# Moving a triangular substitution, its transposes and GpSimd's strip copies in the lead and the first turn of a fused decoder layer

## The chip, the cores and the metric

The kernel runs on one core of a Trainium2 chip. The metric is the device time of one execution in microseconds (us); lower is better.

## The reference

One layer for 512 tokens of width 1024, all in float32. The part at issue is the first of three stages: one projection feeds two token mixers, a differential attention of 8 heads and a chunked gated delta rule of 8 heads (chunks of 64 tokens, keys and values of 128):

```python
proj = rmsnorm(x, attn_norm[i]) @ w_in[i]
qa, ka, va, qb, kb, vb, zb, bb, ab, gl = jnp.split(proj, cuts, axis=-1)
...
probs = softmax(q @ k.T + bias)                  # two of them per head, causal, blocks of 128 rows
w = probs[:, :, 0] - lam * probs[:, :, 1]        # and w @ v
...
kkT = jnp.einsum('nbhid,nbhjd->nbhij', k_beta, k)
A = eye(64) + where(strict, kkT * decay, 0)      # one for each head and chunk: 64 of 64x64
sol = triangular_solve(A, rhs, lower=True, unit_diagonal=True)
...
x = x + (gates0 * (oa @ w_br_a) + gates1 * (ob @ w_br_b)) @ w_out
```

After it come a gated MLP with a short convolution and a gated projection of a per-layer input. The change does not touch them.

## The kernel before

**The projection as filling.** Weights come in chunks of 1024x128 in float32. GpSimd (`both`, L507 and L492) or ScalarE splits each into a high and a low part in a reduced format, and TensorE multiplies it as three products of 512 columns for each of 8 row blocks (`gemm`, L562). One such row block, three products, is one **step**, about 0.68 us. A `Fill` hands steps out, so that the code of TensorE is a list of small products, each behind a number of steps: `f.step(8)`. Four weight buffers turn; GpSimd begins chunk c when the product of chunk c-4 is done.

**Turns.** After the keys of all heads come `lead_turn`, then `turn(0)` to `turn(7)`. `turn(h)` holds the scan of the delta rule for head h and the attention of head h+1 (`a` in the code); `lead_turn` holds the attention of head 0. Each is written out four times, once for TensorE, ScalarE, VectorE and (the projection alone) GpSimd, as a fixed order for that engine; between engines there are only semaphores. Every engine works through its own list in order, so what stands behind a waiting instruction waits too.

**Attention of one head**, in four row blocks i, is a relay. TensorE: `scores(a, i)` (L698, the products of q and k into banks 3 and 4). VectorE: `maxima(a, i)` (L1705 adds the bias, L1710 takes the maxima). ScalarE: `softmax(a, i)` (L1152). VectorE: `combine(a, i)` (L1720 to L1722, the mixed probabilities into `pr`). TensorE: `turn_w(a, i)` (L705, transposes). ScalarE: `keep_w(a, i)` (L1158, into `wT`). `scores(a, i+1)` on TensorE wait for `keep_w(a, i)`. `prep` (L1675) scales q and k of the next head ahead of `scores(a, 0)`.

**The inverses of A.** The 64 matrices are inverted in blocks of 32. First all 128 diagonal blocks of 32x32 by columns on VectorE: `substitute(j0, j1)` does columns j0 to j1-1 of 31, two instructions each (L1810, L1812), and needs nothing from another engine. In the kernel before, the 31 columns are spread over `lead_turn`, between the maxima and the mixing. `turn_back` then transposes the result twice: into `dd` (L1817, semaphore `turned_back` 1) and into `li` (L1819, `turned_back` 2). From `dd` ScalarE places two strips (`place_rows`, L1274), from `li` two more (`place_columns`, L1289) and GpSimd the first two (L523). TensorE computes the blocks below the diagonal, `pair_low` (L756, L758) from `dd`, and, when ScalarE has copied them (`pair_copy`, L1324 and L1325), `pair_high` (L770, L772), from which `pair_sign` (ScalarE) and `pair_turn` (VectorE) fill further strips. Then the 64x64 blocks follow: `half_low(g)` (L785) and `half_high(g)` (L796), 8 matrices to a group, one group in each of turns 0 to 3, with `half_copy` and `half_take` on ScalarE between and behind. `half_take(g)` gives `xf_ready`, for which the first product of the scan of turn g waits (L899).

**GpSimd** copies its strips behind the first chunk that it splits for `stream.heads[0]`, and must wait there for `turned_back` 2:

```python
both(stream.heads[h].at(n))
if h == 0 and n == 0:
    pool.wait_ge(sem("turned_back"), 2)
```

**Two waits that the prediction speaks of.** `first_tap(a, 0)` on ScalarE (L1175) overwrites `qb`, and waits for `qeg`, which VectorE makes from `qb` in `turn` (L1891, behind `at_`, L1889):

```python
if n == 0:
    act.wait_ge(sem("qk"), h)
    act.wait_ge(sem("qeg"), h)
```

SyncE loads the rows for head 1 (`rows_of(1)`) between the second and third chunk of `stream.heads[0]`, and waits there for ScalarE's `first_decay` in the lead.

## Time and profile before

| what | us |
|---|---|
| median of 3 runs (1159.1 to 1159.82) | 1159.25 |
| the profiled execution | 1160.82 |
| its span, first to last instruction | 1159.0 |
| TensorE busy | 1123.9 |
| VectorE busy | 655.2 |
| ScalarE busy | 549.4 |
| GpSimd busy | 633.1 |

Times of the trace below are in the span's own microseconds: the lead begins at about 101 and turn 0 at 149.7. In a row, "[1.82 <-DVE pr L1722]" is the idle time of the engine just before, and what ended it. DVE is VectorE, ACT ScalarE, POOL GpSimd, PE TensorE, PEld its weight loads. A float32 matmul leaves two records, so 8 products show as x16. PEclk is the share of TensorE's full clock that was granted.

### The profile page before, as it was taken

What the parts mean: (1) busy time and instruction counts of PE and PEld (TensorE: products, weight loads), DVE (VectorE), ACT (ScalarE), POOL (GpSimd) and SP (SyncE); (2) the same over time, 40 slices, a digit from 0 to 9 for tenths busy, and PEclk for the clock granted to TensorE, in tenths of its full rate; (3) what the DMA queues carried; (4) which work ended last, traced back from release to release, by engine and by line L of the source; (5) the groups of instructions that cost most, each with busy time, mean ns of one, the idle gap of its engine ahead of it and who ended that gap; (6) DMA issues with size and microseconds to landing.
All of it is one profiled execution on the core that took longest, in us unless ns stands there. A gap on an engine that the chain in (4) does not pass through costs nothing.

```text
span 1159.0 us, 16765 instructions
## 1 busy us (share of the span) xinstructions
PE 1123.9 (97%) x5502; PEld 898.7 (78%) x5502; DVE 655.2 (57%) x1036; ACT 549.4 (47%) x886; POOL 633.1 (55%) x769
## 2 busy tenths in 40 slices
PE   6998989999999999999999999999999999999997
PEld 4786667777777777667878888888888888888886
DVE  4668976767666776862213324476776515731534
ACT  5584647566565656551322124544444314433542
POOL 6386264546554564645456554566576754573452
PEclk9999999999999999999999999999999999999999
DMA  8354031331404123213223523333333432332232
GB/s 243 77 132 130 26 94 35 85 85 35 102 18 118 38 64 100 75 54 85 79 77 105 181 72 91 91 93 114 103 90 91 116 102 73 109 96 80 74 89 79
DMA packets 196619, 104.36 MB, mean 90 GB/s; under 512 B 3926, under 2 KB 195401, under 8 KB 196553
## 3 DMA queue, kind: packets, MB, share of 16 engines
q1 hardware_dynamic: 196172, 103.39, 32.0%
q8 instruction: 34, 0.56, 0.2%
q14 instruction: 32, 0.26, 0.1%
q10 hardware_dynamic: 381, 0.15, 0.1%
HBM read 101.40 MB, written 2.13 MB: 89 GB/s over the span
## 4 chain that ended last, share of the span: by engine, by line
PE 87%; DVE 9%; ACT 3%; issue 1%; ACTq 0%; DVEq 0%
PE bank L562 75%; PE bank L698 2%; PE bank L712 1%; DVE prod L1810 1%; DVE xs L1812 1%; PE bank L705 1%; PE bank L657 1%; DVE pr L1722 1%; PE bank L922 1%; DVE pr L1721 0%; DVE oa_lo L1978 0%; PE bank L909 0%; PE bank L919 0%; PE bank L910 0%; PE bank L913 0%
## 5 line engine op out<-in xcount | busy, mean ns | idle before, releaser
L492 POOL TENSOR_TENSOR w_lo<-w_raw,w_hi 128x256 fp32r<-128x256 f32 x692 | 549.9, 828 | 259.9 <-ACT w_hi L1074 254.2
L562 PE MATMUL bank<-hn_hi,w_hi 128*128 128x512 f32 x1000 | 408.4, 408 | 1.0 <-DVE o_a L1985 1.0
L562 PE MATMUL bank<-hn_hi,w_lo 128*128 128x512 f32 x1000 | 391.0, 391 | 0.0
L562 PE MATMUL bank<-hn_lo,w_hi 128*128 128x512 f32 x1000 | 390.4, 390 | 0.0
L562 PEld LDWEIGHTS bank<-hn_hi,w_hi 128*128 128x128 f32 x1000 | 189.0, 189 | 43.7 <-issue 9.2
L562 PEld LDWEIGHTS bank<-hn_hi,w_lo 128*128 128x128 f32 x1000 | 187.9, 188 | 40.4
L562 PEld LDWEIGHTS bank<-hn_lo,w_hi 128*128 128x128 f32 x1000 | 188.7, 189 | 34.6 <-issue 1.7
L507 POOL CAST w_hi<-w_raw 128x1024 fp32r<-128x1024 f32 x70 | 78.2, 1117 | 222.0 <-PE bank L562 131.3
L1074 ACT ACTIVATE w_hi<-w_raw 128x1024 fp32r<-128x1024 f32 x111 | 117.9, 1062 | 77.6 <-PE bank L562 69.7
L2096 DVE SCALAR_TENSOR_TENSOR u<-vr,pt,u 128x511 f32<-128x511 f32 x88 | 88.9, 1010 | 8.3 <-DVE u L2096 0.7
L2090 DVE TENSOR_TENSOR vr<-bank,rs 128x512 f32<-128x512 f32 x44 | 30.4, 692 | 72.5 <-PE bank L562 67.1
L562 PE MATMUL bank<-fa_hi,w_hi 128*128 128x512 f32 x176 | 68.5, 389 | 0.0
L562 PE MATMUL bank<-fa_lo,w_hi 128*128 128x512 f32 x176 | 68.5, 389 | 0.0
L562 PE MATMUL bank<-fa_hi,w_lo 128*128 128x512 f32 x176 | 68.5, 389 | 0.0
L1536 ACT ACTIVATE u<-vr,pt 128x512 f32<-128x512 f32 x44 | 35.9, 816 | 38.2 <-DVEq L2091 37.5
L2130 DVE TENSOR_TENSOR x<-x,bank 128x512 f32 x16 | 11.0, 688 | 61.2 <-PE bank L562 60.5
L1541 ACT ACTIVATE fa_hi<-tn 128x512 fp32r<-128x512 f32 x22 | 13.9, 633 | 66.4 <-DVE tn L2108 66.4
L1152 ACT ACTIVATE pr<-bank,ast 128x128 f32<-128x128 f32 (+3 forms) x64 | 33.8, 528 | 19.9 <-DVE ast L1710 16.4
L2033 DVE TENSOR_TENSOR sg<-sg,bank 128x512 f32<-128x512 f32 x8 | 5.5, 687 | 62.8 <-PE bank L562 62.8
L1488 ACT ACTIVATE sg<-bank 128x512 f32<-128x512 f32 x12 | 7.2, 599 | 66.3 <-PE bank L562 66.3
L562 PEld LDWEIGHTS bank<-fa_lo,w_hi 128*128 128x128 f32 x176 | 33.0, 188 | 6.9
L562 PEld LDWEIGHTS bank<-fa_hi,w_lo 128*128 128x128 f32 x176 | 33.0, 188 | 6.9
(308 smaller groups left out, 1643.6 us busy)
## 6 DMA issues: line engine op xcount, KB each, us to landing
w_raw<-in_w_in SPq DMA_DIRECT2D x73, 512.0 KB, 6.7
w_raw<-in_w_up SPq DMA_DIRECT2D x44, 512.0 KB, 3.8
w_raw<-in_w_down SPq DMA_DIRECT2D x16, 512.0 KB, 3.9
crow<-cum_rows_out SPq DMA_DIRECT2D x16, 256.0 KB, 5.7
w_raw<-in_w_br_a SPq DMA_DIRECT2D x8, 512.0 KB, 4.0
w_raw<-in_w_br_b SPq DMA_DIRECT2D x8, 512.0 KB, 4.0
w_raw<-in_w_out SPq DMA_DIRECT2D x8, 512.0 KB, 3.9
w_raw<-in_w_ple_gate SPq DMA_DIRECT2D x8, 512.0 KB, 4.0
```

The source lines that it names most:

```text
L492: ins = pool.tensor_tensor(wlo[c.slot][:, ks, :], raw[c.slot][:, ks, :], whi[c.slot][:, ks, :].bitcast(F32), ALU.subtract)
L507: pool.tensor_copy(whi[c.slot][:, :, :], raw[c.slot][:, :, :]).then_inc(high_ready, 1)
L562: mm = pe.matmul(acc, w[c.slot][:, i, :], xx[:, x0 + i, :], start=(i == 0 and n == 0), stop=last)
L657: mm = pe.matmul(tiles(b)[:, t, :], key(h)[:, s], key(h)[:, s], start=True, stop=True)
L698: mm = pe.matmul(bank[3 + j][:, 0:(i + 1) * P], qa[s, i * P:(i + 1) * P], ka[s, 0:(i + 1) * P], start=True, stop=True)
L705: mm = pe.transpose(bank[3][:, t * P:(t + 1) * P], pr[0][:, t * P:(t + 1) * P], ident)
L1074: done(nc.scalar.activation(whi[c.slot][:, :, :], raw[c.slot][:, :, :], ACT.Copy), high_ready, c.number + 1)
L1152: done(nc.scalar.activation(pr[j][:, 0:w], bank[3 + j][:, 0:w], ACT.Exp, bias=ast[:, 2 + j:3 + j], scale=-1.0, accum_out=ast[:, 4 + j:5 + j]),
L1536: done(nc.scalar.activation(u[:, :], v[:, :], ACT.Identity, bias=col(PA_FBIAS + q * KF, f), scale=col(PA_TAP[2] + q * KF, f)), "u_made", 2 ...
L1541: done(nc.scalar.activation(fa_hi[:, 8 * FFN_HALF[part] + pair, :], tn[:, :], ACT.Copy), "fa_hi", f + 1)
L2090: done(V.tensor_tensor(v[:, :], bank[c.bank][:, :], rs[:, :], ALU.mult), bank_free[c.bank], c.uses + 1)
L2096: link(V.scalar_tensor_tensor(out=u[:, back:], in0=v[:, 0:T - back], scalar=col(PA_TAP[j] + q * KF, f), in1=u[:, back:], op0=ALU.mult, op1 ...
```

## The change

Four things, in one edit.

1. VectorE in the lead: `prep(0, 1)` goes ahead of the last instruction of `scale_rows`; the columns are spread behind the maxima with fewer in the lead (22 of 31), and the other 9 go into turn 0, around combine(1,0). `first_mask` goes behind `prep(1, 1)`.
2. VectorE in turn 0: maxima(1,0) come first; the transpose into `dd` comes behind column 30, maxima(1,1) ahead of the transpose into `li`; `at_` and `qeg` come behind both. The pair transposes and `key_decays(0)` go behind combine(1,2). TensorE's pair products, and ScalarE's strips and copies, move back in turn 0 accordingly, and `STEPS_FIRST` and the first steps of the lead are set anew.
3. Halves: the low half of group g+1 and the high half of group g are issued alternately in one group, `halves(g)`: `halves(-1)` and `halves(0)` in turn 0, then one in each of turns 1 to 3. `halves(3)` has the high half alone.
4. GpSimd's two strip copies go behind the fourth chunk of `stream.heads[0]`.

```diff
-STEPS_FIRST = ((2, 4, 1, 9, 1, 8, 1, 8), ((1, 1), (1, 1, 1), (1, 1, 1), (1, 1, 1)))
+STEPS_FIRST = ((2, 4, 1, 10, 1, 8, 1, 7), ((1, 1), (1, 1, 1), (1, 1, 1), (1, 1, 1)))
...
             for h in range(H - 2):
                 for n in range(len(TURN)):
                     both(stream.heads[h].at(n))
-                    if h == 0 and n == 0:
+                    if h == 0 and n == 3:
                         pool.wait_ge(sem("turned_back"), 2)
-                        pool.wait_ge(low_ready, stream.heads[0].at(0).number + 1)
+                        pool.wait_ge(low_ready, stream.heads[0].at(3).number + 1)
...
+            def low_half(m):
+                b = (5, 7)[m // 8 % 2]
+                at = slice(m % 8 * HEAD, (m % 8 + 1) * HEAD)
+                return pe.matmul(bank[b][UP, at], lt6[LOW, m, :], xf[LOW, m, UP], start=True, stop=True)
+
+            def high_half(m):
+                b = (5, 7)[m // 8 % 2]
+                at = slice(m % 8 * HEAD, (m % 8 + 1) * HEAD)
+                return pe.matmul(bank[b][LOW, at], lt6[UP, m, :], xf[UP, m, UP], start=True, stop=True)
+
+            def halves(g):
+
+                pe.wait_ge(sem("placed"), 2 if g < 0 else 6)
+                pe.wait_ge(sem("pairs"), 1 if g < 1 else 2)
+                if g >= 0:
+                    pe.wait_ge(sem("inverse_ui"), g + 3)
                 if g > 0:
                     pe.wait_ge(sem("ob_sum_read"), g)
                 for n in range(8):
-                    m = g * 8 + n
-                    mm = pe.matmul(bank[b][UP, n * HEAD:(n + 1) * HEAD], lt6[LOW, m, :], xf[LOW, m, UP],
-                                   start=True, stop=True)
-                mm.then_inc(sem("inverse_u"), 1)
...
+                    if g < H // 2 - 1:
+                        low = low_half(8 * g + 8 + n)
+                    if g >= 0:
+                        high = high_half(8 * g + n)
+                if g < H // 2 - 1:
+                    low.then_inc(sem("inverse_u"), 1)
+                if g >= 0:
+                    high.then_inc(sem("inverse_x"), 1)
```

TensorE's `lead_turn` and `turn`:

```diff
-                f.step(1)
+                f.step(2)
                 scores(0, 0)
                 f.step(6)
                 turn_w(0, 0)
...
-                f.step(before[1] - 2 if h == 0 else before[1])
+                f.step(before[1])
                 if h > 0 and halves_ob(h - 1):
...
-                if h == 0:
-                    for g in range(2):
-                        pair_low(g)
-                        f.step(1)
                 if attention:
                     turn_w(a, 0)
                 f.step(before[2])
                 if attention:
                     scores(a, 1)
+                if h == 0:
+                    f.step(6)
+                    pair_low(0)
+                    f.step(1)
+                    pair_low(1)
+                    f.step(2)
...
                 mm.then_inc(sem("vb_T"), 1)
-                if h == 0:
-                    f.step(before[3] - 5)
-                    pair_high(0)
-                    f.step(2)
-                    pair_high(1)
-                    f.step(3)
-                else:
-                    f.step(before[3])
+                f.step(before[3] - 9 if h == 0 else before[3])
                 if attention:
                     turn_w(a, 1)
                 f.step(before[4])
                 if attention:
                     scores(a, 2)
                     k_turn(a)
...
-                if h < H // 2:
-                    half_low(h)
-                f.step(before[5])
+                if 0 < h < H // 2:
+                    halves(h)
+                if h == 0:
+                    f.step(1)
+                    pair_high(0)
+                    f.step(2)
+                    pair_high(1)
+                    f.step(before[5] - 3)
+                else:
+                    f.step(before[5])
                 if attention:
                     turn_w(a, 2)
-                if h < H // 2:
-                    half_high(h)
                 f.step(before[6])
                 if attention:
                     scores(a, 3)
-                f.step(before[7])
+                if h == 0:
+                    f.step(3)
+                    halves(-1)
+                    f.step(3)
+                    halves(0)
+                    f.step(before[7] - 6)
+                else:
+                    f.step(before[7])
                 if more_a:
                     qk_sum(h + 2, 0, at("qa"))
```

ScalarE's `lead_turn` and `turn`:

```diff
                 prep_v(1, at("va"))
-                place_rows()
...
                     ob_r(h - 1)
-                if h == 0:
-                    pair_copy(0)
...
                     first_tap(a, 0, at("qb"))
                     softmax(a, 1)
                     if h == 0:
+                        place_rows()
+                        pair_copy(0)
+                        pair_copy(1)
+                    keep_w(a, 1)
+                    silu_exp(a, 0)
+                    if 0 < h < H // 2 - 1:
+                        half_copy(h + 1)
+                    if 0 < h < H // 2:
+                        half_take(h)
+                    softmax(a, 2)
+                    if h == 0:
                         pair_sign(0)
                         pair_sign(1)
-                    keep_w(a, 1)
-                    if h == 0:
+                        keep_w(a, 2)
                         place_columns()
-                    silu_exp(a, 0)
-                    if h < H // 2:
-                        half_copy(h)
-                    softmax(a, 2)
                     first_tap(a, 2, at("vb"))
                     head_exps(a)
-                    keep_w(a, 2)
-                    if h < H // 2:
-                        half_take(h)
+                    if h > 0:
+                        keep_w(a, 2)
                     k_copy(a)
+                    if h == 0:
+                        half_copy(0)
                     if more_a:
                         prep_qk(h + 2, 0, at("qa"))
                     square_q(a)
                     softmax(a, 3)
+                    if h == 0:
+                        half_copy(1)
+                        half_take(0)
                     silu_exp(a, 2)
                     keep_w(a, 3)
                     v_copy(a)
```

VectorE's `scale_rows`, `turn_back`, `lead_turn` and `turn`:

```diff
                 V.tensor_copy(wide(xs)[:, 0:SUB * SUB:SUB + 1], kzb[:, :])
+                prep(0, 1)
                 link(V.tensor_tensor(li[:, :, :], li[:, :, :], kzb[:, :].unsqueeze(2).to_broadcast([P, SUB, SUB]), ALU.mult))
...
                 done(V.transpose(dd[:, :, 0:SUB].rearrange("p n c -> p c n"), xs[:, :, :].rearrange("p i c -> p c i")),
                      "turned_back", 1)
+
+            def turn_again():
+
                 done(V.transpose(li[:, :, :].rearrange("p n i -> p i n"), xs[:, :, :]), "turned_back", 2)
...
-                prep(0, 1)
-                substitute(0, 3)
                 maxima(0, 0)
-                substitute(3, 5)
+                substitute(0, 2)
                 combine(0, 0)
-                substitute(5, 8)
+                substitute(2, 4)
                 maxima(0, 1)
-                substitute(8, 10)
+                substitute(4, 6)
                 combine(0, 1)
                 steps(conv(0, 0, at("qb")))
                 maxima(0, 2)
-                substitute(10, 12)
+                substitute(6, 8)
                 combine(0, 2)
                 steps(conv(0, 2, at("vb")))
                 maxima(0, 3)
                 steps(finish_silu(0, 0))
-                substitute(12, 13)
+                substitute(8, 9)
                 combine(0, 3)
-                substitute(13, 18)
+                substitute(9, 14)
                 prep(1, 0)
-                substitute(18, 24)
+                substitute(14, 20)
                 steps(finish_silu(0, 2))
                 attention_scale(0)
-                substitute(24, 28)
+                substitute(20, 21)
+                prep(1, 1)
+                substitute(21, 22)
                 first_mask()
-                prep(1, 1)
-                substitute(28, 31)
-                turn_back()
...
+                if h == 0:
+                    maxima(a, 0)
+                    substitute(22, 24)
+                    combine(a, 0)
+                    substitute(24, 31)
+                    turn_back()
+                    maxima(a, 1)
+                    turn_again()
+                    scaled_keys()
+                    combine(a, 1)
+                    scaled_values()
+                else:
+                    if attention:
+                        maxima(a, 0)
+                    if halves_ob(h - 1):
+                        low_ob(h - 1)
+                    scaled_keys()
...
-                    maxima(a, 0)
-                if h > 0 and halves_ob(h - 1):
-                    low_ob(h - 1)
...
-                if attention:
-                    combine(a, 0)
-                else:
-                    low_a(range(5, 7))
-                if h > 0:
-                    key_decays(h)
-                if attention:
-                    maxima(a, 1)
-                    if h > 0:
...
-                if attention:
-                    combine(a, 1)
+                    steps(conv(a, 0, at("qb")))
+                    maxima(a, 2)
+                    steps(finish_silu(a, 0))
+                    combine(a, 2)
                     if h == 0:
                         pair_turn(0)
                         pair_turn(1)
                         key_decays(h)
-                    steps(conv(a, 0, at("qb")))
-                    maxima(a, 2)
-                    steps(finish_silu(a, 0))
-                    combine(a, 2)
                     steps(conv(a, 2, at("vb")))
                     maxima(a, 3)
```

How the order moves on VectorE, at the end of the substitution and the beginning of turn 0. Before (L1810 and L1812 are a column, L1817 and L1819 the transposes, L1705 and L1710 maxima, L1720 to L1722 the mixing):

```order
L1810 TENSOR_TENSOR prod<-li,xs 128x31
L1812 TENSOR_TENSOR xs<-xs,prod 128x31
L1817 STREAM_TRANSPOSE dd<-xs 128x32x32
L1819 STREAM_TRANSPOSE li<-xs 128x32x32
L1705 TENSOR_TENSOR bank<-bank,bias 128x128 x2
L1710 TENSOR_REDUCE ast<-bank 128x1 x2
L1889 TENSOR_TENSOR at_<-bank,dec 128x512
L1891 TENSOR_TENSOR qeg<-qb,eg 128x512
L1720 RECIPROCAL ast<-ast 128x2
L1721 TENSOR_SCALAR pr<-pr,ast,sm 128x128
L1722 SCALAR_TENSOR_TENSOR pr<-pr,ast 128x128
L1705 TENSOR_TENSOR bank<-bank,bias 128x256 x2
```

Now (L1828 and L1830 a column, L1835 and L1840 the transposes, L1722 and L1727 maxima, L1737 to L1739 the mixing, L1905 and L1907 `at_` and `qeg`):

```order
L1828 TENSOR_TENSOR prod<-li,xs 128x60
L1830 TENSOR_TENSOR xs<-xs,prod 128x2x30
L1828 TENSOR_TENSOR prod<-li,xs 128x31
L1830 TENSOR_TENSOR xs<-xs,prod 128x31
L1835 STREAM_TRANSPOSE dd<-xs 128x32x32
L1722 TENSOR_TENSOR bank<-bank,bias 128x256 x2
L1727 TENSOR_REDUCE ast<-bank 128x1 x2
L1840 STREAM_TRANSPOSE li<-xs 128x32x32
L1905 TENSOR_TENSOR at_<-bank,dec 128x512
L1907 TENSOR_TENSOR qeg<-qb,eg 128x512
L1737 RECIPROCAL ast<-ast 128x2
L1738 TENSOR_SCALAR pr<-pr,ast,sm 128x256
```

`at_` and `qeg` stood between maxima(1,0) and combine(1,0), and stand now behind maxima(1,1) and both transposes, just ahead of combine(1,1).

ScalarE, from the first strips to the second kept row block. Before (L1274 `place_rows`, L1324 and L1325 pair copies, L1158 `keep_w`, L1175 `first_tap`, L1152 softmax):

```order
L1274 ACTIVATE o_a<-dd 32x32x32 x2
L1152 ACTIVATE pr,ast<-bank,ast 128x128 x2
L1324 ACTIVATE dd<-bank 32x16x32
L1325 ACTIVATE dd<-bank 32x16x32
L1324 ACTIVATE dd<-bank 32x16x32
L1325 ACTIVATE dd<-bank 32x16x32
L1158 ACTIVATE wT<-bank 128x128
L1200 ACTIVATE zb<-bank 128x512
L1203 ACTIVATE silu<-bank 128x512
L1163 ACTIVATE silu<-silu,sm 128x512
L1164 ACTIVATE silu<-silu 128x512
L1175 ACTIVATE qb<-bank,pt 128x512
```

Now, from the tap on (L1186 `first_tap`, L1163 softmax, L1285 `place_rows`, L1335 and L1336 pair copies, L1169 `keep_w(1, 1)`):

```order
L1186 ACTIVATE qb<-bank,pt 128x512
L1163 ACTIVATE pr,ast<-bank,ast 128x256 x2
L1285 ACTIVATE o_a<-dd 32x32x32 x2
L1335 ACTIVATE dd<-bank 32x16x32
L1336 ACTIVATE dd<-bank 32x16x32
L1335 ACTIVATE dd<-bank 32x16x32
L1336 ACTIVATE dd<-bank 32x16x32
L1169 ACTIVATE wT<-bank 128x2x128
L1202 ACTIVATE silu<-qb 128x512
L1174 ACTIVATE silu<-silu,sm 128x512
L1175 ACTIVATE silu<-silu 128x512
L1163 ACTIVATE pr,ast<-bank,ast 128x384 x2
```

The strips and the pair copies stood ahead of `keep_w(1, 0)`, and stand now between softmax(1,1) and `keep_w(1, 1)`.

## Rows read from the trace of the kernel before

**Rows 1.** The page, busy time of the engines.

```profile
PE 1123.9 (97%) x5502; PEld 898.7 (78%) x5502; DVE 655.2 (57%) x1036; ACT 549.4 (47%) x886; POOL 633.1 (55%) x769
```

**Rows 2.** Waits of PE, 60 to 151 us: total, times, longest.

```profile
PE bank L705 <- DVE pr L1722: 3.3, 2, 1.8
PE bank L698 <- DVE ka L1675: 1.9, 2, 1.1
```

**Rows 3.** Timeline of PE: start, us, engine, line.

```profile
149.69 0.49 PE L698 MATMUL bank<-ka,qa 64*128 64x128 f32 x4 [0.83 <-DVE ka L1675]
...
160.17 0.33 PE L705 MATMUL bank<-sq,pr 128*128 128x128 f32 x1 [2.09 <-DVE pr L1722]
```

**Rows 4.** Windows: length, busy PE, PEld, DVE, ACT, POOL, PEclk, DMA share, GB/s.

```profile
140.00:151.00 11.00, 10.17 (x44) 7.35 (x43) 10.07 (x28) 5.32 (x9) 0.00 (x0) 1.00 0.62 168
...
153.90:155.10 1.20, 1.14 (x64) 1.09 (x64) 0.00 (x0) 1.17 (x2) 1.00 0.00 0
...
160.00:161.00 1.00, 0.83 (x4) 0.66 (x4) 0.11 (x1) 0.45 (x3) 1.00 (x2) 0.79 0.00 0
161.00:164.00 3.00, 3.00 (x11) 1.75 (x10) 1.11 (x4) 2.34 (x4) 2.92 (x5) 0.50 0.20 48
```

**Rows 5.** Timeline of DVE, columns 22 to 30 and the mask between.

```profile
142.28 0.38 DVE L1810 TENSOR_TENSOR prod<-li,xs 128x207 f32<-128x207 f32 x1
...
148.16 0.69 DVE L1830 TENSOR_TENSOR dec<-dec,sq 128x512 f32<-128x512 f32 x1
...
150.98 0.19 DVE L1812 TENSOR_TENSOR xs<-xs,prod 128x31 f32<-128x31 f32 x1
```

**Rows 6.** Timelines of DVE and of POOL in the lead.

```profile
100.65 1.58 DVE L1675 SCALAR_TENSOR_TENSOR ka<-ka_raw,pt,sqr 128x512 f32<-128x512 f32 x1
...
111.47 0.79 DVE L1812 TENSOR_TENSOR xs<-xs,prod 128x192 f32<-128x192 f32 x1
...
143.50 0.36 DVE L1812 TENSOR_TENSOR xs<-xs,prod 128x192 f32<-128x192 f32 x1
...
111.30 2.95 POOL L492 TENSOR_TENSOR w_lo<-w_raw,w_hi 128x256 fp32r<-128x256 f32 x4
...
155.60 2.12 POOL L523 COPY o_a<-li 32x1024 f32<-32x1024 f32 x2 [26.64 <-DVE li L1819]
```

**Rows 7.** Timelines of DVE and of ACT, turn 0.

```profile
151.20 2.32 DVE L1817 STREAM_TRANSPOSE dd<-xs 128x1024 f32<-128x1024 f32 x1
...
157.35 0.91 DVE L1891 TENSOR_TENSOR qeg<-qb,eg 128x512 f32<-128x512 f32 x1
...
163.65 0.76 DVE L1710 TENSOR_REDUCE ast<-bank 128x1 f32<-128x256 f32 x2
...
153.62 2.15 ACT L1274 ACTIVATE o_a<-dd 32x1024 f32<-32x1024 f32 x2 [7.45 <-DVE dd L1817]
...
158.88 0.59 ACT L1324 ACTIVATE dd<-bank 32x512 f32<-32x512 f32 x1
...
164.73 0.69 ACT L1175 ACTIVATE qb<-bank,pt 128x512 f32<-128x512 f32 x1 [1.33 <-PE bank L562]
...
166.42 0.19 ACT L1152 ACTIVATION_READ_ACCUMULATOR pr<-bank,ast 128x1 f32 x1
```

**Rows 8.** Timeline of PE: scores(1,2), and the first product of the scan.

```profile
173.67 0.92 PE L698 MATMUL bank<-ka,qa 64*128 64x384 f32 x4
...
191.39 0.38 PE L899 MATMUL bank<-vbt,o_a 128*128 128x128 f32 x2
```

**Rows 9.** Timeline of PE: turn 1 (first two rows) and turn 4.

```profile
232.22 0.49 PE L705 MATMUL bank<-sq,pr 128*128 128x128 f32 x3
...
234.60 0.70 PE L698 MATMUL bank<-ka,qa 64*128 64x512 f32 x2
...
385.37 0.49 PE L705 MATMUL bank<-sq,pr 128*128 128x128 f32 x3
...
386.50 0.70 PE L698 MATMUL bank<-ka,qa 64*128 64x512 f32 x2
```

49 lines of the change are left out of this document (24 added, 25 removed).

## The prediction

> **What bounds the kernel now.** I read the page first: TensorE is busy for 97% of the span [rows 1], so a change that only orders work anew can win no more than TensorE's idle time, its time at the lower clock, and matmuls that are made shorter. Second, the waits of TensorE up to 151 us: two for the mixed probabilities (`combine`, L1722; 3.3 us) and two for `ka` (`prep`, L1675; 1.9 us), all in the lead or just before and behind it [rows 2]. The reader is to see that all of them wait for VectorE. The timeline then has one more, 2.09 us before the transpose of 160.17 [rows 3], and behind it TensorE is granted 0.79 of its clock from 160 to 161 and 0.50, the lower of its two levels, from 161 to 164 [rows 4]. That costs 0.2 + 1.5 = 1.7 us more. So 5.2 us in the lead and 3.8 us in turn 0 are to be had, 9 us or 0.8%. Third, VectorE's own time, in the windows: from 140 to 151 us it is busy for 10.07 of 11 [rows 4]. The lead is as long as VectorE's work in it.
>
> **1. The lead.** If no wait is left, scores(1,0) stand at 149.69 - 5.2 = 144.5 [rows 3]. They need `prep(1, 1)`, which ends at 149.63. Ahead of it the change takes away columns 22 to 27 of the substitution and the mask. Column 22 begins at 142.28, and its two instructions and the two of column 23 take 1.61 us; the eight of 24 to 27 end at 148.16 and take 2.76, and the six of 28 to 30, 1.53, end at 151.17 [rows 5]; so 24 to 30 are 4.29 us, and 22 to 27 4.37. With the mask (0.7) that is 5.1 us, so `prep(1, 1)` could end at 144.5 as well: no wait at all.
>
> But the change also lets GpSimd run. Before, it stands for 26.6 us until it can copy the strips [rows 6], and is idle while VectorE substitutes. Now it splits three more chunks (the second to fourth of `stream.heads[0]`) in the lead and at its end. The trace shows what that does: a column's subtraction of 128x192 takes 0.79 us beside GpSimd's split and 0.36 us without it, so **0.43 us for each instruction with both operands in SBUF** [rows 6]. The second chunk becomes free under combine(0,3) and the first columns behind it: about 4 such instructions, 1.7 us. The third and the fourth land when the rows for head 1 are through the queue, in the stretch of 140 to 151 us less some 4 [rows 4]: they meet `finish_silu`, column 20 and `prep(1, 1)`, five instructions, 2.0 us. Against this the front of the lead is relieved: `prep(0, 1)`, column 7 and combine(0,1) no longer fall on a split, which I put at 3.0 us (`prep(0, 1)` took 1.58 us beside a split [rows 6] and the same `ka` 0.75 without one, 148.88 to 149.63, and I give the other two 1.1 each); and with fewer columns between them VectorE waits for scores for about 1.5 us in all. Sum: 144.5 + 1.7 + 2.0 - 3.0 + 1.5 = 146.7 us. scores(1,0) come 3.0 us earlier than before, with a wait of 2.2 us in place of 5.2. Bounds: 144.5 (none of the three chunks hurts) and 148.7 (no relief, two instructions more).
>
> The Trainium skill has a rule here that speaks against this change (SBUF — State Buffer, "Who interferes with whom"): the pair of ports that VectorE and GpSimd share is locked for a whole instruction by whoever begins first, and the other waits. The trace agrees that they collide, but shows 0.43 us, not the 0.74 us of a whole split instruction (2.95 us for four) [rows 6].
>
> **2. Turn 0, up to scores(1,2).** VectorE from 146.7: column 21 (0.84), mask (0.7), maxima(1,0) (1.0), columns 22 and 23 (1.61), combine(1,0) (0.96), columns 24 to 30 (4.29), and 1.7 for four instructions beside the last chunk: 157.8. From there a chain without slack, in which the new order puts three engines in a row [rows 5, 7]: transpose to `dd` 2.35 with its gap, maxima(1,1) 1.55 (twice 0.76), the second transpose 2.0 (the two end at 155.54 before), `at_` and `qeg` 1.65 (0.7 + 0.91); ScalarE's `first_tap(1, 0)` waits for `qeg` (it overwrites `qb`), and softmax(1,1) stands behind it in its queue: 1.9 from the start of the one to the end of the other; then, before it keeps the turned probabilities, `place_rows` 2.2 (two copies) and four pair copies at 0.59, 2.4; `keep_w(1, 1)` 0.4. That is 14.4 us, and TensorE's scores(1,2) wait for it: 172.2. TensorE's own work from the first transpose is some 9.5 us, so it loses about 5 us here, at the turn of (1,1) and at scores(1,2), in two pieces; ahead of that about 0.9 at the turn of (1,0) and 0.9 at the first pair product.
>
> Before, scores(1,2) stand at 173.67 [rows 8], with the two high pair products (1.2 each) done and one step of the projection (0.68) fewer. At equal work that is 173.67 - 2.4 + 0.7 = 172.0. **The turn's gain from the lead is used up: +0.2 us.** The old order hid this: `qeg` was made ahead of combine(1,0), and `place_rows` ran while ScalarE had nothing to do.
>
> **3. Turn 0, the rest.** From scores(1,2) to the turn of (1,2) there is TensorE's own work, 9.6 us with the pair products. Then ScalarE keeps those probabilities, places two strips (2.2), and only then takes the first tap of `vb`; VectorE's convolution (2.3) and maxima(1,3) (2.1) follow, softmax(1,3) ends about 10.7 us behind the turn, and `half_copy(1)` and `half_take(0)` (0.6 each) stand behind it. `xf_ready` comes 12.0 us after the turn, TensorE wants it after 10.0: **+2.0 us**, and +0.4 for combine(1,3). Before, `half_take(0)` was long done, and the first product of the scan stood at 191.39, 17.7 us behind scores(1,2) [rows 8], with no wait. Bounds of this step: +0.5 and +3.5.
>
> **4. Halves alternated.** Turns 1 to 3 lose one group of 64x64 products each (turns 1 and 2 carry two groups as one, turn 3 has only the high half left). What a group costs is read from two turns: 2.38 us between the turn of the third row block and the fourth scores with it, 1.13 without it [rows 9]. So 3 x 1.25 = 3.75 us, if a group of both halves is as long as one. For this speaks that the 64 records of a 32x32 pair group, on two tiles in turn, take 1.14 us [rows 4], 18 ns each, with 32 columns moved at a time; a group of 64x64 has 16 records on one tile in about the same time. The halves use different rows, different columns and different banks. If they did not overlap, each of the three merged groups (turns 0, 1 and 2) would cost another 1.07: 3.75 - 3.2 = 0.5 us. I take **-3.75**; no wait stands close ahead of those places that would swallow it (combine is done 0.9 us before).
>
> **5. The clock.** The old loss of 1.7 us lies in the 173.67 of step 2. The new waits before scores(1,2) leave TensorE with little work for six microseconds; it fell to 0.50 before after small pair products and a wait of 2.09 us [rows 3, 4]. What it loses up to scores(1,2) is covered by the waits; behind them it is between 0 and 1.7. I take +0.8.
>
> **Sum.** +0.2 + 2.4 - 3.75 + 0.8 = **-0.3 us** against the profiled execution (1159.0 span, 1160.82 in all, which is 1.6 above the median of the runs, 1159.25). So **1159.0 us**. What a measurement can tell from no change is 0.2%, 2.3 us: 1156.9 and 1161.6. That the change does not do what it says is excluded by the order of the instructions, which shows each move.
>
> **The rivals.**
> - *GpSimd's chunks hardly hurt* (0.34). If its splits fall beside maxima, convolutions and transposes, which read PSUM or one operand and keep their time beside it, scores(1,0) stand at 144.5 and VectorE is another 2 us earlier at the transposes: -4.4 on the sum, 1154.6 us. For it: VectorE has only a few such instructions at any time. Against it: the third and fourth chunk land where substitution is nearly all it does.
> - *The halves do not overlap* (0.13). The sum loses 3.2: 1162.2 us, slower. It decides itself in turn 1: a merged group that takes over 1.6 us. For it: each product loads its own weights. Against it: the pairs.
> - *Whole instructions blocked* (0.15), slower. Each of the 13 instructions of VectorE that I let meet a split waits for a whole one of 0.74 us [rows 6] instead of 0.43: 13 x 0.31 = 4.0 us, less some 0.8 where TensorE has slack. The transposes begin at 161, and everything behind them, which has no slack, moves by 3.2 us: 1162.2 us. It decides where combine(0,3) ends: after 132 us it holds. Against it: the 0.79 us of column 7. The Trainium skill's rule of the lock (SBUF — State Buffer, "Who interferes with whom") is this case.
> - The forecast itself (0.38), with a range of its own of 1157 to 1161.3.
>
> **The numbers.** Faster by over 0.2% 0.34, within 0.2% 0.38, slower 0.28. The range reaches to the first and to the slow rivals: 1154.4 to 1162.6.
>
> **What would show it.** In the new trace: (1) no wait at the first two turns of the lead, and 1.5 to 3 us at scores(1,0), at 146 to 148 us; (2) GpSimd busy between 127 and 150, and columns 9 to 21 beside it at 0.8 us; (3) about 3 us of wait at the turn of (1,1) for L1739, the counterpart of L1722, and 2 us at scores(1,2) for `keep_w`, with low clock at 166 to 175; (4) 2 us for `half_take(0)` at the first product of the scan of turn 0; (5) merged groups of 1.1 us. Wrong, if scores(1,2) come before 168 us (then the gain is real), if (5) is 2.1, or if the sum of TensorE's waits up to 200 us is under 6 us.

## The result: 0.27% slower, and the profile after

The changed kernel takes **1161.6 us** (median of 12 runs, 1159.99 to 1164.13); the kernel before, on the same chip, 1159.07 (12 runs, 1157.58 to 1160.2). The ratio is 1.0027, with a 95% interval of 1.0019 to 1.0034: slower by about 2.5 us. The forecast was 1159.0 and no measurable change. The profiled execution has a span of 1161.9 us.

TensorE's busy time on the page is what it was [rows 1]:

```profile
PE 1124.0 (97%) x5502; PEld 897.2 (77%) x5502; DVE 656.6 (57%) x1036; ACT 549.6 (47%) x886; POOL 636.2 (55%) x769
```

The waits of TensorE, of 60 to 151 us, for the kernel after (total, times, longest). They answer to [rows 2]; 5.2 us have become 3.3:

```profile
PE bank L698 <- DVE ka L1692: 1.9, 1, 1.9
PE bank L705 <- DVE pr L1739: 1.4, 3, 0.9
```

The same view of 151 to 217 us. The kernel before has 3.1 us there, all for VectorE: the 2.09 us of [rows 3], and 1.0 us that already lies in its turn 1, which begins at 209.02:

```profile
PE bank L705 <- DVE pr L1739: 4.4, 3, 2.3
PE bank L698 <- ACT wT L1169: 2.1, 1, 2.1
PE bank L910 <- ACT o_a L1306: 1.3, 1, 1.3
```

The timeline of TensorE after (start, us, line), which answers to [rows 3, 8]. From the top: scores(1,0), the turns of (1,0) and (1,1), scores(1,2), the first product of the scan, scores(2,0):

```profile
147.02 0.38 PE L698 MATMUL bank<-ka,qa 64*128 64x128 f32 x2 [1.88 <-DVE ka L1692]
...
154.65 0.33 PE L705 MATMUL bank<-sq,pr 128*128 128x128 f32 x1 [1.90 <-DVE pr L1739]
...
170.35 0.44 PE L705 MATMUL bank<-sq,pr 128*128 128x128 f32 x2 [2.25 <-DVE pr L1739]
...
173.57 1.01 PE L698 MATMUL bank<-ka,qa 64*128 64x384 f32 x2 [2.08 <-ACT wT L1169]
...
196.44 0.38 PE L910 MATMUL bank<-vbt,o_a 128*128 128x128 f32 x1 [1.26 <-ACT o_a L1306]
...
216.23 0.38 PE L698 MATMUL bank<-ka,qa 64*128 64x128 f32 x2
```

Windows of the kernel after (length, busy PE, PEld, DVE, ACT, POOL, PEclk, DMA share, GB/s). The kernel before has one stretch at the lower clock in turn 0 [rows 4]; this one has three, and in each 4 x 0.43 = **1.7 us** of TensorE's work at full clock are lost:

```profile
156.00:160.00 4.00, 4.00 (x14) 2.97 (x11) 3.62 (x12) 1.83 (x3) 0.00 (x0) 0.57 0.03 9
173.00:177.00 4.00, 3.43 (x11) 2.08 (x11) 2.07 (x5) 2.46 (x5) 2.42 (x4) 0.57 0.00 0
197.00:201.00 4.00, 3.83 (x16) 3.54 (x17) 1.95 (x5) 3.81 (x7) 0.00 (x0) 0.57 0.00 0
```

Timelines of VectorE and ScalarE after, the chain that [rows 7] had in the old order: the two transposes, softmax behind `first_tap`, then `place_rows` and `keep_w(1, 1)`:

```profile
158.92 2.30 DVE L1835 STREAM_TRANSPOSE dd<-xs 128x1024 f32<-128x1024 f32 x1
...
162.84 2.00 DVE L1840 STREAM_TRANSPOSE li<-xs 128x1024 f32<-128x1024 f32 x1
...
166.59 0.69 ACT L1186 ACTIVATE qb<-bank,pt 128x512 f32<-128x512 f32 x1 [8.70 <-DVE qeg L1907]
167.31 0.47 ACT L1163 ACTIVATE pr<-bank,ast 128x256 f32<-128x256 f32 x1
...
168.51 2.14 ACT L1285 ACTIVATE o_a<-dd 32x1024 f32<-32x1024 f32 x2
...
173.13 0.38 ACT L1169 ACTIVATE wT<-bank 128x256 f32<-128x256 f32 x1
```

**Where the time went**, read from the starts of the scores of each head. Head 1 comes 2.7 us earlier (147.02 against 149.69). Not all of that is the lead's. The first products of L657, which stand ahead of all that the change touches, are at 42.69 against 43.43, and the kernel before has a stretch at the lower clock in its opening that this profile lacks. Its window, then the same window after:

```profile
17.00:21.00 4.00, 3.46 (x13) 3.06 (x14) 3.82 (x6) 3.81 (x7) 3.92 (x6) 0.57 0.32 79
17.00:21.00 4.00, 3.33 (x18) 2.47 (x18) 3.81 (x6) 3.81 (x6) 3.92 (x6) 1.00 0.44 109
```

So 0.7 us come from the opening, where the thirteen profiles differ by chance (the same products stand at 41.7 to 44.3), and 1.9 from what lies between, where the change works. Turn 0 then lasts 69.2 us against 59.3 (it ended at 209.02), 9.9 more, with the same 48 steps of the projection in both kernels. Of the 9.9, TensorE's idle time is 5.7 (7.8 against 2.1) and its busy time 4.2, of which the three stretches at the lower clock against one are about 3.3; the other 0.9 is not explained. Turns 1 to 3 are shorter by 1.36, 1.24 and 1.23. At the scores of head 5 the new kernel stands at 415.94 against 412.53, and from there to its end it is 0.5 us shorter, which is not explained either.

### The profile page after: what moved, and what is told of

It is laid out like the page before. It is cut to its first block, busy times and chain, and to the rows that moved or that the text cites. A ratio compares the mean times of both kernels' runs of the same rounds, so it can differ in the third digit from the quotient of the medians.

```text
span 1161.9 us, 16765 instructions
## 1 busy us (share of the span) xinstructions
PE 1124.0 (97%) x5502; PEld 897.2 (77%) x5502; DVE 656.6 (57%) x1036; ACT 549.6 (47%) x886; POOL 636.2 (55%) x769
## 4 chain that ended last, share of the span: by engine, by line
PE 85%; DVE 9%; ACT 3%; issue 1%; DMA 1%; SPq 0%; DVEq 0%; ACTq 0%
PE bank L562 74%; PE bank L698 2%; PE bank L712 1%; DVE prod L1828 1%; DVE xs L1830 1%; DVE pr L1739 1%; PE bank L705 1%; PE bank L657 1%; DMA x_tok<-in_x 1%; PE bank L933 1%; DVE hn_lo L1648 1%; ACT pr L1163 1%; DVE pr L1738 1%; DVE oa_lo L2015 0%; PE bank L920 0%
## 5 line engine op out<-in xcount | busy, mean ns | idle before, releaser
L1163 ACT ACTIVATE pr<-bank,ast 128x128 f32<-128x128 f32 (+3 forms) x64 | 33.9, 529 | 25.4 <-DVE ast L1727 21.3
L562 PEld LDWEIGHTS bank<-fa_hi,w_hi 128*128 128x128 f32 x176 | 33.0, 188 | 6.9
```

The source lines that it names most:

```text
L562: mm = pe.matmul(acc, w[c.slot][:, i, :], xx[:, x0 + i, :], start=(i == 0 and n == 0), stop=last)
L1163: done(nc.scalar.activation(pr[j][:, 0:w], bank[3 + j][:, 0:w], ACT.Exp, bias=ast[:, 2 + j:3 + j], scale=-1.0, accum_out=ast[:, 4 + j:5 + j]),
```

## The experiments

Two theories. **Clock**: the forecast's waits are about right, and what made the kernel slower is that TensorE, after them, is granted the lower clock more often. **Waits alone**: turn 0's chain is what counts, and the low clock lies beside waits. The comparisons below are ratios to the kernel before, run on the same chip in turn; its medians were 1159.07 us for the change, 1159.58 for the next four, 1159.88 for the four behind them and 1158.47 for the last three. A ratio is the recorded one and can differ by up to 0.001 from that of the two medians.

| kernel | median, us | ratio | 95% interval |
|---|---|---|---|
| the change | 1161.6 | 1.0027 | 1.0019 to 1.0034 |
| halves_alone | 1157.12 | 0.9975 | 0.9965 to 0.9985 |
| act_ahead | 1156.71 | 0.9973 | 0.9961 to 0.9985 |
| columns_early | 1164.65 | 1.0044 | 1.003 to 1.0057 |
| act_all | 1158.09 | 0.9986 | 0.9977 to 0.9995 |
| clock_held | 1159.9 | 1.0003 | 0.9994 to 1.0012 |
| serial_halves | 1164.53 | 1.0038 | 1.0025 to 1.0051 |
| strips_third | 1163.38 | 1.0038 | 1.0026 to 1.0051 |
| ahead_third | 1154.24 | 0.9961 | 0.9949 to 0.9974 |
| strips_first | 1165.76 | 1.0062 | 1.0049 to 1.0076 |
| ahead_first | 1165.85 | 1.0062 | 1.0048 to 1.0076 |
| third_held | 1158.16 | 0.9997 | 0.9988 to 1.0006 |

### The halves alone

The kernel before with part 3 of the change and nothing else. `halves(0)` takes the place of `half_high(0)`, and ScalarE's copies move with it; the cut shows the first place.

```diff
 # turn, TensorE, in the kernel before
-                if h < H // 2:
-                    half_low(h)
+                if h == 0:
+                    halves(-1)
+                elif h < H // 2:
+                    halves(h)
```

> The kernel before with part 3 of the change alone: low and high halves alternated, everything else in the old order. If the two halves run beside each other, turns 1 to 3 are each shorter by 1.25 us (as the trace of the changed kernel has it: 50.3 against 51.5 us), and the time is 3.8 us under the kernel before, 1155.3 us. If they run one after another, it is within 0.6 us of the kernel before.

Measured: 1157.12 us, ratio 0.9975, 2.9 us faster where 3.8 were expected. In its profile turns 1 to 3 are shorter by 1.22, 1.20 and 1.24 us, 3.7 in all, as expected, and turn 0 is 0.8 longer. So this part wins, and **the other three parts together lose**: from 0.9975 to 1.0027 is 0.0052, 6.0 us. The forecast had +3.4 for them.

### The halves one behind the other

```diff
-                for n in range(8):
-                    if g < H // 2 - 1:
+                if g < H // 2 - 1:
+                    for n in range(8):
                         low = low_half(8 * g + 8 + n)
-                    if g >= 0:
+                if g >= 0:
+                    for n in range(8):
                         high = high_half(8 * g + n)
```

> The changed kernel with the eight low products of a merged half group issued ahead of its eight high ones, as before, instead of in turns; places, copies and waits are those of the changed kernel. If the turns are what makes the group short (products on the two diagonal quarters of the array overlap), each of the three merged groups of turns 1 to 3 takes its 1.25 us longer again: 1161.6 + 3.75 = 1165.3 us, and turns 1 to 3 last 51.5 us each as in the kernel before. Rival (the group is short because it is one group in one place, in whatever order): 1161.6, turns of 50.25 us.

Both theories missed. Timeline of TensorE, scores and turn of the third row block in turn 1, in the changed kernel:

```profile
231.18 0.92 PE L698 MATMUL bank<-ka,qa 64*128 64x384 f32 x4
...
239.31 0.49 PE L705 MATMUL bank<-sq,pr 128*128 128x128 f32 x3
```

and here:

```profile
232.28 0.92 PE L698 MATMUL bank<-ka,qa 64*128 64x384 f32 x4
...
241.12 0.49 PE L705 MATMUL bank<-sq,pr 128*128 128x128 f32 x3
```

8.13 us against 8.84. In turn 3 of the changed kernel, where the group has only the high half, the stretch takes 8.12:

```profile
331.69 0.59 PE L698 MATMUL bank<-ka,qa 64*128 64x384 f32 x2
...
339.81 0.49 PE L705 MATMUL bank<-sq,pr 128*128 128x128 f32 x3
```

So in turns the second half is **free** (8.13 against 8.12), and one behind the other it costs 0.71 us. By subtraction, the 1.25 us that a group costs in a place of its own [rows 9] are 0.71 for its products and 0.54 for one more interruption of the stream of large products, which joining alone saves. The medians cannot carry this by themselves: the total moved by 0.0011 in the ratio, 1.3 us, not by the 3.75 expected, and the intervals overlap.

### TensorE kept busy in its waits

```diff
-                for t in range(NT):
-                    s = slice(t * P, (t + 1) * P)
-                    mm = pe.matmul(tiles(6)[:, t, :], key(h)[:, s], qb[:, s], start=True, stop=True)
+                for again in range(3 if h == 0 else 1):
+                    for t in range(NT):
+                        s = slice(t * P, (t + 1) * P)
+                        mm = pe.matmul(tiles(6)[:, t, :], key(h)[:, s], qb[:, s], start=True, stop=True)
```

and the same around the transposes of vb (5 times), `turn_w(1, 1)` (9) and the first pair of gate products of head 2 (3).

> The changed kernel, in which TensorE repeats products that give the same numbers again while it would wait in turn 0: the four QK products three times instead of once, the four transposes of vb five times, the transposes of turn_w(1,1) nine times, the first pair of the gate products of head 2 three times. Nothing else is touched, so VectorE's and ScalarE's chains are as in the changed kernel. The theory (the lower clock of the three stretches 156 to 160, 173 to 177 and 197 to 201 us is what turned the gain into a loss): the granted clock is 1.00 all through turn 0. The first of the three stretches lies ahead of turn_w(1,1), which waits 2.25 us for VectorE, so its 1.7 us turn into a longer wait; the second and the third (1.7 us each) lie where TensorE sets the time. So scores(2,0) starts 2 to 3.4 us earlier than 216.2, and the time is 1158.2 to 1159.6 us, middle 1159.0, against 1161.6. Rival (the waits alone set the time; the stretches at the lower clock lie beside other waits): 1161.0 to 1162.0, with the same start of scores(2,0). Second rival (the repeats run into the path, since they do not fit in the waits): above 1162.5.

Measured: 1159.9 us, ratio 1.0003; the intervals of this and of the change do not overlap, and 0.0024 is **2.8 us won by more work**. The stretches behind 153 us are gone; one stood ahead of them, behind the wait for scores(1,0), which nothing fills:

```profile
149.00:153.00 4.00, 4.00 (x22) 3.81 (x21) 3.79 (x9) 0.92 (x4) 3.92 (x5) 0.57 0.48 131
153.00:217.00 64.00, 62.18 (x589) 48.17 (x588) 44.07 (x85) 39.11 (x70) 26.84 (x31) 1.00 0.21 55
```

VectorE's chain did not move against scores(1,0) by more than 0.1 us (its second transpose starts 15.84 us behind them, against 15.82), and head 2 begins 66.1 us behind head 1 in place of 69.2: 3.1 us less, in the range expected, though the median, 1159.9, is 0.3 above its own. That is the clock theory; "the waits alone" would have left both as they were.

A profile is one execution, but every run has its mean granted clock on record, to 0.001. One minus it, times the span, is the time lost to the clock in that run. Averaged over the runs it is 7.0 us for the change (12 runs), 4.0 for this kernel (11 runs) and 5.6 for the kernel before (52 runs, 5.1 to 6.2 by batch). The repeats took out 3.0 us of loss and 2.8 us of time, which bears the clock theory out beyond the single profile. It also limits it: against the kernel before the change loses only 1.4 us more by this count, so not all of its 2.5 us are shown to be the clock's, and this kernel, with less loss than the kernel before, is still no faster than it.

### Less contention, and the clock again

```diff
-                    if h == 0 and n == 3:
+                    if h == 0 and n == 2:
                         pool.wait_ge(sem("turned_back"), 2)
-                        pool.wait_ge(low_ready, stream.heads[0].at(3).number + 1)
+                        pool.wait_ge(low_ready, stream.heads[0].at(2).number + 1)
```

> The changed kernel with GpSimd's two strips behind its third chunk of head 0 instead of behind the fourth, so that one chunk is not split beside VectorE's columns (in the changed kernel from 148.3 to 153.0 us) but behind the strips. Theory (each VectorE instruction on two operands in SBUF beside a split costs 0.43 us more, four of them here): the second transpose of VectorE starts 1.7 us earlier than 162.8, turn_w(1,0) and turn_w(1,1) with it, scores(1,2) at 171.9 instead of 173.6, and the time is 1159.9 us; one of the stretches at the lower clock may go with the shorter wait, which would give 1158.5. Rival (the chunk that is now split behind the strips comes too late for its products): a wait of TensorE for w_lo or w_hi, above 1162 us. Rival (contention costs nothing there): 1161.6.

The time did not fall: ratio 1.0038. But the chain did get shorter. Scores(1,2) stand at 170.11, not 173.57; of these 3.5 us only 1.7 are the chain's, from the first scores of head 1 on (24.89 us against 26.55), as much as expected. The other 1.8 lie ahead of head 1 and are not this edit's: 0.5 by the first scores of head 0, and 1.3 in the lead, which takes 44.7 us here and in the profiles of clock_held, serial_halves and columns_early too, whose strips are where the change has them, against 46.0 in the changed kernel.

```profile
145.22 0.38 PE L698 MATMUL bank<-ka,qa 64*128 64x128 f32 x2 [1.88 <-DVE ka L1692]
...
166.89 0.44 PE L705 MATMUL bank<-sq,pr 128*128 128x128 f32 x2 [3.10 <-DVE pr L1739]
...
170.11 1.01 PE L698 MATMUL bank<-ka,qa 64*128 64x384 f32 x2 [2.08 <-ACT wT L1169]
```

No wait for a weight appears, so the late chunk is not the cause. What came behind ate the gain: windows of the same kernel show the lower clock nearly throughout from 168 to 179 us, and again at 196. Over single microseconds that is 5.1 and 1.7 us lost, 0.7 of them in the wait ahead of 170.11.

```profile
168.00:171.00 3.00, 0.92 (x5) 0.51 (x4) 1.84 (x3) 2.86 (x6) 2.92 (x5) 0.62 0.56 145
171.00:175.00 4.00, 4.00 (x47) 2.56 (x45) 2.48 (x5) 2.36 (x6) 3.92 (x6) 0.50 0.08 24
175.00:179.00 4.00, 4.00 (x53) 2.90 (x50) 2.31 (x4) 1.27 (x3) 1.46 (x2) 0.50 0.02 4
196.00:200.00 4.00, 3.96 (x17) 3.63 (x18) 1.92 (x4) 3.73 (x6) 0.00 (x0) 0.57 0.00 0
```

This edit with the repeats of clock_held tells the two apart:

> The kernel with the strips behind the third chunk (1163.4 us; 6.8 us were lost to a lower clock in its turn 0, 168 to 179 and 196 to 200 us) with the repeated products of clock_held, which fill TensorE's waits in turn 0. Theory (its VectorE chain is shorter by 3 us than the changed kernel's, and the clock took that back): no stretch at the lower clock between 165 and 205 us, and 1163.4 - 5 = 1158.5 us, middle of 1157.5 to 1159.5, that is, faster than the 1159.9 of clock_held too. Rival (it is the late chunk, not the clock): 1163.4, or above.

Measured: 1158.16 us, ratio 0.9997, 0.0041 (4.8 us) below strips_third, as expected. The mean loss to the clock over the runs falls with it, from 10.1 us (6 runs) to 3.2 (11 runs). From 150 to 215 us the granted clock is full:

```profile
145.00:150.00 5.00, 5.00 (x27) 4.45 (x24) 4.65 (x13) 0.92 (x4) 1.06 (x2) 0.66 0.44 119
150.00:215.00 65.00, 64.16 (x599) 49.77 (x597) 45.37 (x86) 39.27 (x71) 33.34 (x37) 1.00 0.21 54
```

That it beats clock_held, as expected too, the intervals do not show; its chain is shorter by the 1.7 us said above, not by 3.

### ScalarE's order

```diff
 # turn, ScalarE, behind maxima(1, 1)
-                    first_tap(a, 0, at("qb"))
-                    softmax(a, 1)
-                    if h == 0:
-                        place_rows()
-                        pair_copy(0)
-                        pair_copy(1)
+                    if h > 0:
+                        first_tap(a, 0, at("qb"))
+                    else:
+                        place_rows()
+                    softmax(a, 1)
+                    if h == 0:
+                        pair_copy(0)
+                        pair_copy(1)
+                        first_tap(a, 0, at("qb"))
```

> The changed kernel with ScalarE's list in turn 0 set differently: place_rows, softmax(1,1) and both pair copies ahead of first_tap(1,0), which waits for qeg. Theory (the relay through ScalarE's queue): the 2.25 us before the turn of (1,1) and the 2.08 us before scores(1,2) go, and the dip of the clock behind them (174 to 177 us, 1.5 us) with them: about 5.5 us under the changed kernel, 1156 us. Rival (VectorE's list is as late anyway, or GpSimd's splits in the lead are what costs): under 2 us of gain.

Measured: 1156.71 us, ratio 0.9973, as expected, though by another sum. ScalarE no longer stands for 8.7 us behind `qeg`; its timeline:

```profile
161.13 2.15 ACT L1285 ACTIVATE o_a<-dd 32x1024 f32<-32x1024 f32 x2 [3.43 <-DVE dd L1838]
163.31 0.47 ACT L1163 ACTIVATE pr<-bank,ast 128x256 f32<-128x256 f32 x1
...
166.96 0.69 ACT L1186 ACTIVATE qb<-bank,pt 128x512 f32<-128x512 f32 x1
```

and TensorE no longer waits at scores(1,2):

```profile
168.62 0.44 PE L705 MATMUL bank<-sq,pr 128*128 128x128 f32 x2 [1.61 <-DVE pr L1742]
...
169.69 0.59 PE L698 MATMUL bank<-ka,qa 64*128 64x384 f32 x2
```

Head 2 begins 62.4 us behind head 1, 6.8 less than in the change. TensorE is idle there for 5.7 us in place of 7.8, and busy for 56.7 in place of 61.4; the three stretches at the lower clock, 5.1 us, are all absent (PEclk 1.00 from 145 to 215 us). They were not all on the path. The first, at 156, lay ahead of the wait of 2.25 us for VectorE and only shortened it. Up to scores(1,2) the kernel is 3.7 us shorter (22.86 against 26.55 from the first scores of head 1), which is the shorter chain, and behind them 3.1, which is about what the two stretches there cost. So **nearly half of what the order gave came through the clock.**

The order at the other place of ScalarE that I had named, `place_columns` and `first_tap(1, 2)` ahead of `keep_w(1, 2)`:

```diff
-                        keep_w(a, 2)
                         place_columns()
                     first_tap(a, 2, at("vb"))
+                    if h == 0:
+                        keep_w(a, 2)
```

> The changed kernel with place_columns and first_tap(1,2) ahead of keep_w(1,2) on ScalarE in turn 0. Theory: VectorE's convolution of vb no longer stands for 4.7 us, half_take(0) comes in time, the waits of 1.3 and 0.3 us before the scan go, and the dip of the clock at 197 to 201 us (1.7 us) with them: about 3 us under the changed kernel, 1158.5 us. Rival (half_take is late for another reason, the many copies behind it): under 1 us.

A miss: 1164.65 us, no gain. `first_tap(1, 2)` did come 3.8 us earlier, 1.0 of it because head 1 did; the wait at the scan is 1.5 us and not less. ScalarE then stands for the low products of `halves(-1)`, which TensorE reaches behind scores(1,3):

```profile
184.07 0.69 ACT L1186 ACTIVATE vb<-bank,pt 128x512 f32<-128x512 f32 x1
...
189.93 0.59 ACT L1342 ACTIVATE lt<-bank 64x512 f32<-64x512 f32 x1 [3.25 <-PE bank L779]
```

Softmax(1,3) and `half_take(0)` stand behind that in its queue. The median above the change's own is not explained by this profile, whose span, 1161.5 us, is no longer than the changed kernel's; the intervals overlap. The mean loss to the clock over its five runs is 8.8 us against 7.0, so the clock is the likely reason; why it fell more often is not shown.

Both orders together:

> The changed kernel with both reorderings of ScalarE's list. Theory: the two gains add, 8 to 8.5 us under the changed kernel, about 1153.3 us, which is below the kernel before and below halves_alone. Rival: after the first is mended the second has slack anyway or a new wait takes its place, and the gain is 6 us or less.

Measured: 1158.09 us, a miss: no better than the first order by itself, with intervals that overlap. It is 4.8 us under the change by the ratios, where the rival had "6 us or less". In its profile a wait of 0.8 us at scores(1,2) is back, and two stretches at the lower clock, at 156 and 194 us.

### The first order and the strips together

act_ahead's edit with that of strips_third.

> Both: place_rows, softmax(1,1) and the pair copies ahead of first_tap(1,0) on ScalarE in turn 0 (which alone gave 1156.7 us), and GpSimd's strips behind its third chunk. If the 1.7 us of contention were still on the path to turn_w(1,1): 1155.0 to 1155.5 us. Rival (turn 0's waits behind turn_w(1,1) take the gain back): 1156.7. Rival (the late chunk is waited for): above 1157.5.

Measured: **1154.24 us, ratio 0.9961 (0.9949 to 0.9974)**, below what was expected, and faster than either kernel. That it beats halves_alone (0.9965 to 0.9985) or act_ahead, the intervals do not show, so it is not shown either that parts 1, 2 and 4 give anything beyond part 3, even in their best form. TensorE waits only 1.28 us at the turn of (1,1), and not at scores(1,2):

```profile
166.60 0.44 PE L705 MATMUL bank<-sq,pr 128*128 128x128 f32 x2 [1.28 <-DVE pr L1742]
```

Set against strips_third, from which only the order on ScalarE differs, it is 9.1 us faster. The profiles say of what: from the first scores of head 0 to those of head 2 it is 8.9 us shorter. In turn 0 TensorE is idle for 4.8 us less and busy for 4.3 less; the loss at the lower clock is 5.1 less, 0.7 of which lay within the wait ahead of 170.11.

### Where the strips must not stand

The same edit with `n == 0` and `at(0)`, the old place:

> The changed kernel with GpSimd's strips back behind its first chunk of head 0, so that the three chunks after it are not split beside VectorE's columns but behind the strips, at some 160 to 175 us. Theory (0.43 us for each VectorE instruction on two operands in SBUF that lies beside a split): the lead and the columns shorten, VectorE's second transpose starts 3 to 5 us earlier than 162.8, and the start of scores(1,2) comes forward by as much, less what combine(1,1) and the copies around it lose beside the splits that now lie there (about 1 us); as in the kernel with the strips behind the third chunk, the longer wait ahead of turn_w(1,1) may bring stretches at the lower clock (1.7 us each) that take it back: 1159 to 1163 us. If there is no such stretch: 1157.5. Rival (the three late chunks are waited for): waits of TensorE for w_hi or w_lo, above 1163.

> The same with place_rows, softmax(1,1) and the pair copies ahead of first_tap(1,0) on ScalarE (that order with the strips behind the third chunk gave 1154.2 us, the best so far). Theory: the columns lose 1.7 to 3 us more of contention, turn_w(1,1) does not wait, and what is gained is kept in part: 1152 to 1154. Rival (the splits behind the strips now slow combine(1,1) and what follows as much as they slowed the columns): 1154 to 1156. Rival (the late chunks are waited for): above 1158.

Measured: 1165.76 and 1165.85 us, the slow rival in both. The contention is gone from the lead (scores(1,0) at 144.42 with no wait), but the timeline of TensorE in strips_first has this row:

```profile
165.51 0.79 PE L562 MATMUL bank<-hn_hi,w_hi 128*128 128x512 f32 x1 [13.04 <-POOL w_lo L492]
```

GpSimd, its timeline says, stands until VectorE's last transpose, and then has the strips and the chunk still to do:

```profile
158.81 2.47 POOL L523 COPY o_a<-li 32x1024 f32<-32x1024 f32 x2 [34.68 <-DVE li L1840]
161.34 1.04 POOL L507 CAST w_hi<-w_raw 128x1024 fp32r<-128x1024 f32 x1
162.46 3.00 POOL L492 TENSOR_TENSOR w_lo<-w_raw,w_hi 128x256 fp32r<-128x256 f32 x4
```

With the transposes moved back, part 4 of the change is therefore a condition of part 2, and its price is the contention.

## Why the prediction was wrong

The steps in their order.

1. *The lead.* The start is right, in part by luck: 146.7 forecast, 147.02 measured. The wait at scores(1,0) is 1.88 us, but "no wait" was forecast for the turns ahead of it, and they have 1.4; in all 3.3 against 2.2. What made up for it is the opening, 0.7 us earlier by chance. (The upper bound of 148.7 was also added wrongly: without relief the terms give 149.7 before any further instruction.)

The price of contention, 0.43 us, was read from one instruction. It holds for most columns, but the instruction just ahead of it in the kernel before lost 0.71 us (1.07 against the 0.36 of the same shape at 143.10), and the mask in the kernel after lost 0.72 (0.69 without a split). The lines, the first from the kernel before:

```profile
110.36 1.07 DVE L1810 TENSOR_TENSOR prod<-li,xs 128x192 f32<-128x192 f32 x1
```

and these from the kernel after; the last two show the same instruction one column apart, beside a split and behind it:

```profile
148.67 1.41 DVE L1851 TENSOR_TENSOR dec<-dec,sq 128x512 f32<-128x512 f32 x1
...
151.65 0.79 DVE L1830 TENSOR_TENSOR xs<-xs,prod 128x207 f32<-128x207 f32 x1
...
153.27 0.36 DVE L1830 TENSOR_TENSOR xs<-xs,prod 128x192 f32<-128x192 f32 x1
```

The Trainium skill's rule of the lock (SBUF — State Buffer, "Who interferes with whom") would have the instruction stand for a whole one of GpSimd's. The trace shows a collision, but no such fixed price: 0.40 to 0.42 us for the columns beside a split, 0.07 for one of them, and 0.72, nearly a whole split instruction of 0.74, for the mask.

2. *Turn 0 up to scores(1,2).* Right in its mechanism: both waits are there, in the places named. The columns ended 1.1 us late (158.9, forecast 157.8), the chain behind them took 14.6 us (forecast 14.4), so scores(1,2) came at 173.57, not 172.2: **1.4 us under**. Of the 1.1, 0.3 is the later start. The rest is contention: I had charged 1.7 us to the last chunk, and VectorE's timeline has five column instructions beside it and the mask, which took 1.41 us in place of 0.69 [rows 5]; 2.4 us in all.

3. *The rest of turn 0.* The half was ready when forecast: the first product of the scan stands 11.8 us behind the turn of (1,2), forecast 12.0. The wait there was smaller, 1.26 us against 2.0, only because TensorE's own work up to it took 10.6 us and not 10.0; with 0.25 against 0.4 for combine(1,3), this step is 0.3 over. I took `place_columns` for the cause of the wait; columns_early shows that it was not.

4. *Halves.* Right, -3.8 us against -3.75, and the overlap is real: complete, where the forecast only needed "as long as one". That serial_halves lost 1.3 us and not 3.2 was wrong: I had taken the place of a group as free.

5. *The clock.* **This step failed.** "What it loses up to scores(1,2) is covered by the waits; behind them it is between 0 and 1.7. I take +0.8." There were two stretches behind them, one behind scores(1,2), one behind the wait at the scan: 3.4 us, of which 0.1 lies in the wait itself, so 3.3. That is 2.5 us over what I took, and outside my bounds. I had looked for the cost of a wait at one place, though step 3 itself forecast another wait of the same size. Two experiments show that the term is real and about this large: more work in the same waits made the kernel 2.8 us faster, and strips_third, with its shorter chain, 4.8.

At the scores of head 2 the forecast was 209.02 + 3.4 = 212.4, and they stand at 216.23, 3.8 later: 1.4 of step 2, 2.5 of step 5, and -0.1 for all else. From there to the end the profiles differ from the forecast by another -0.6 (halves -0.1, the rest of the kernel -0.5, not explained). So the forecast of -0.3 became +2.9 in the spans of the profiles and +2.5 in the medians; the size of single terms is known from one pair of profiles only.

Of the rivals none came. No chunk was free. The halves do overlap. The lock did not cost a whole instruction each time, and combine(0,3) ended at 131.2, not behind 132. The slower side was reached by a term that I had priced only inside the forecast. The signs that the forecast named for being wrong did not catch it: scores(1,2) came behind 168, merged groups took 1.1 us, and the waits up to 200 us are 11.1 us and not under 6. None of them looked at the clock behind the waits.

## What to carry to other kernels

A wait in an engine that is otherwise full has two prices: its own length, and the stretch at the lower clock that may follow, here 1.7 us for a wait of about 2. An earlier start of a relay is worth nothing where the relay then waits: shorten the chain first (here by ScalarE's order), and only then move work into the gap. Where small products on different quarters of the array are pending, issue them in turns and in one place.

## What the runs showed that I had not expected

- The loss per stretch is the same nearly everywhere: 1.7 us in the change, in act_all, in ahead_third, 3.4 where two follow one another (columns_early) and 5.1 where three do (strips_third, serial_halves). But a wait does not decide it. act_ahead has waits of 1.86, 1.93 and 1.61 us and no such stretch in turn 0; the changed kernel, in the same code up to there, has one at 156 us. The opening, the same code in all thirteen kernels, has one in five of the profiles and none in eight. So a single profile shows one draw, and the medians and the mean clocks of all runs, not the profiles, carry the verdicts.
- A second half group in turns with the first costs nothing: 8.13 us against 8.12. Why three of these stretches joined in strips_third and not in the change is open.
